# Splitting the first two rows of four residual stages during the stage before, and reserving their accumulators one by one

## The reference, cut to what matters

```python
h = h + mixed @ w_out                                         # "out":  16 rows of 128 inputs
h = h + (silu(v @ w_ffn_gate) * (v @ w_ffn_up)) @ w_ffn_down  # "down": 44 rows
...
h = h + mix @ w_out_2                                         # "out2": 16 rows
h = h + memory_cross_attention(...)                           # "xo":    4 rows
h = h + peer(...)                                             # "v0" and "v1": 64 rows each
```

## Time and profile before

| What | Value |
|---|---|
| runs shown | 4111.41, 4116.86, 4119.94 us; median 4116.86 |
| profiled execution, its own time | 4109.78 us |
| its span in the trace | 4108.1 us |
| PE busy | 3978.6 us, 97% |
| DVE busy | 2362.7 us, 58% |
| ACT busy | 2064.1 us, 50% |
| chain of work that ended last | PE 94%, DVE 3%, ACT 2%, issue 1% |
| rows in the six residual stages | 208 |

### The profile page before, as it was taken

The page is one execution under the profiler, slowest core; times in us unless marked ns, Lnnn a source line. Parts: engine busy times, 40 slices in busy tenths (PEclk is TensorE's granted clock), DMA queues, the critical chain, the costliest instruction groups (busy, mean ns, idle before and its releaser), DMA issues.

```text
span 4108.1 us, 82547 instructions
## 1 busy us (share of the span) xinstructions
PE 3978.6 (97%) x33876; PEld 3930.4 (96%) x33876; DVE 2362.7 (58%) x3414; ACT 2064.1 (50%) x3097; POOL 33.4 (1%) x61
## 2 busy tenths in 40 slices
PE   7999999999999998999999998999999999999998
PEld 6999999999999998999999898999999999999998
DVE  5655565554444456444665665897765555554555
ACT  6555554455555444444554444447764444444443
POOL 0000000000000000000000000000000000000000
PEclk9999999999999999999999999999999999999999
DMA  4545555545555554543335443555555556665553
GB/s 174 175 165 175 174 178 182 175 162 191 191 191 193 183 194 148 175 165 134 134 125 184 155 173 124 185 195 180 179 192 191 192 193 215 214 214 179 191 193 132
DMA packets 111188, 726.08 MB, mean 177 GB/s; under 512 B 11296, under 2 KB 11424, under 8 KB 29184
## 3 DMA queue, kind: packets, MB, share of 16 engines
q1 hardware_dynamic: 105904, 701.55, 49.8%
q0 software_dynamic: 5072, 21.50, 1.6%
HBM read 712.52 MB, written 10.49 MB: 176 GB/s over the span
## 4 chain that ended last, share of the span: by engine, by line
PE 94%; DVE 3%; ACT 2%; issue 1%; DMA 0%; DVEq 0%; SPq 0%; ACTq 0%
PE ps L493 19%; PE ps L501 19%; PE ps L494 19%; PE ps L550 9%; PE ps L552 9%; PE ps L557 9%; PE ps L580 1%; PE ps L981 1%; PE ps L615 1%; PE ps L522 1%; PE ps L523 1%; PE ps L524 1%; ACT wh L1043 1%; PE ps L633 1%; DVE tmp L1661 1%
## 5 line engine op out<-in xcount | busy, mean ns | idle before, releaser
L1602 DVE TENSOR_TENSOR wl<-raw,wh 128x1024 fp32r<-128x1024 f32 x1328 | 1616.8, 1225 | 1509.7 <-ACT wh L1043 1505.1
L1043 ACT ACTIVATE wh<-raw 128x1024 fp32r<-128x1024 f32 x1328 | 1402.9, 1060 | 1770.3 <-PE ps L550 625.1
L493 PE MATMUL ps<-x,wh 128*128 128x256 f32 x6784 | 1620.0, 281 | 41.6 <-DVE x L1655 25.1
L494 PE MATMUL ps<-x,wh 128*128 128x256 f32 x6784 | 1604.2, 278 | 0.0
L493 PEld LDWEIGHTS ps<-x,wh 128*128 128x128 f32 x6784 | 1283.9, 189 | 51.2 <-issue 44.8
L494 PEld LDWEIGHTS ps<-x,wh 128*128 128x128 f32 x6784 | 1283.6, 189 | 0.6
L501 PE MATMUL ps<-x,wl 128*128 128x256 f32 x6784 | 919.0, 278 | 2.9 <-DVE wl L1602 2.9
L501 PEld LDWEIGHTS ps<-x,wl 128*128 128x128 f32 x6784 | 843.2, 189 | 3.2 <-DVE wl L1602 3.1
L550 PE MATMUL ps<-xkh,wh 128*128 128x256 f32 x3328 | 783.7, 278 | 29.1 <-DVE xkl L1613 27.2
L552 PE MATMUL ps<-xkl,wh 128*128 128x256 f32 x3328 | 783.2, 278 | 0.0
L550 PEld LDWEIGHTS ps<-xkh,wh 128*128 128x128 f32 x3328 | 630.4, 189 | 30.1 <-issue 30.1
(11 more groups left out here) (340 smaller groups left out, 2190.4 us busy)
## 6 DMA issues: line engine op xcount, KB each, us to landing
raw<-in_w_in SPq DMA_DIRECT2D x184, 1024.0 KB, 4.8
raw<-in_expert_u SPq DMA_DIRECT2D x128, 1024.0 KB, 4.8
raw<-in_expert_v SPq DMA_DIRECT2D x128, 1024.0 KB, 4.8
raw<-in_w_ffn_gate SPq DMA_DIRECT2D x44, 1024.0 KB, 4.7
raw<-in_w_ffn_up SPq DMA_DIRECT2D x44, 1024.0 KB, 4.8
raw<-in_w_ffn_down SPq DMA_DIRECT2D x44, 1024.0 KB, 4.8
raw<-in_w_out SPq DMA_DIRECT2D x32, 1024.0 KB, 4.8
raw<-in_w_branch SPq DMA_DIRECT2D x16, 1024.0 KB, 4.9
```

The costliest lines, as they stand in the source:

```text
L493: begin(mm(o, wh[:, j, c], x_h[:, kc, :], start=kc == 0, stop=False), kc % 8 == 0)
L494: mm(o, wh[:, j, c], x_l[:, kc, :], start=False, stop=False)
L1043: f(wh[:, u % 4, 0:width], raw[:, ring, c:c + width], ACT.Copy).then_inc(*k.up("hi"))
L1602: v.tensor_tensor(wl[:, u % 4, 0:width], raw[:, ring, c:c + width], wh[:, u % 4, 0:width].bitcast(F32), ALU.subtract).then_inc(*k.up("lo"))
```

## The change

- `residual` on ACT and DVE takes `early=True` for `out`, `down`, `out2` and `v1`: the split of rows 0 and 1 is left out there, and a new function `early_rows` does it sooner. ACT's version waits for a new semaphore, `early_ready`, which DVE sets once some tile before the last is complete.
- `out`: DVE sets the flag before the last quarter (q = 3). ACT splits after the fourth gate tile, DVE ahead of the multiplications of `mix_in(3, 3)`. Banks of this last tile are filled and read in the order 3, 4, 5, 7. The two weight halves of this `mix_in` move behind the second and the fourth bank. The flag `masks_free` moves behind the residual stage.
- `down` and `v1`: the last turn of the loops `ffn` and `u1` on ACT and DVE is written out, and the split is in its last tile: on ACT after the gate of `ffn`, and before the last tile of `u1`; on DVE after the third (`ffn`) or first (`u1`) weight half of the last tile. In `ffn` DVE's fourth half goes behind the multiplication.
- `out2`: DVE sets the flag after `mixed_b(6)`, ahead of `scaled(1)`. ACT splits before the weight halves of u = 7, DVE before its first half of u = 7; its second half goes behind `mixed_b(7)`.
- PE (all six residual stages): instead of all eight banks ahead of the first row, each bank is reserved just before its first matmul.
- `xo` and `v0` keep the late split.

```diff
+        def mix_banks(n, q):
+
+            return (3, 4, 5, 7) if (n, q) == (3, 3) else (7, 4, 5, 3)
...
-                parts_T([(b, Y_AT[n], 4) for b in (7, 4, 5, 3)])
-                marks["wb", n, q] = k.n["full_v3"]
+                parts_T([(b, Y_AT[n], 4) for b in mix_banks(n, q)])
+                marks["wb", n, q] = k.n[f"full_v{mix_banks(n, q)[-1]}"]
...
+                        if first and t % 2 == 0:
+                            reserve(t // 2)
...
-                reserve(*range(8))
                 rows(True, False)
...
-            def residual(src, name, n, more=True, between=None):
-                act.wait_ge(*k.next("src_ready"))
+            def early_rows(src):
+
+                act.wait_ge(*k.next("early_ready"))
                 for j in range(2):
                     xsplit(src, j, k.at("hi", -4))
+
+            def residual(src, name, n, more=True, between=None, early=False):
+                act.wait_ge(*k.next("src_ready"))
+                if not early:
+                    for j in range(2):
+                        xsplit(src, j, k.at("hi", -4))
...
                     gate(3, 4 * q + t)
+                if q == 3:
+                    early_rows(mix1)
                 mixed_in(3, q)
-            residual(mix1, "out", KC)
+            residual(mix1, "out", KC, early=True)
...
                     flag("gate_ready")
+                    if last and n == 1:
+                        early_rows(hidT)
                     done_v(4 + n, i + (marks["ffn"][n] + 1))
-            residual(hidT, "down", FT)
+
+            with k.loop("ffn", act, FT // 2 - 1) as i:
+                unit_turn(i)
+            unit_turn(FT // 2 - 1, True)
+            residual(hidT, "down", FT, early=True)
...
             for u in range(4, 8):
+                if u == 7:
+                    early_rows(mix2)
                 up_done(u)
...
+                    if last and j == 7:
+                        early_rows(ag)
                     done(b)
...
-                half()
+                last = (n, q) == (3, 3)
+                if last:
+                    early_rows(mix1)
+                else:
+                    half()
                 dve.wait_ge(*k.next("gate_ready"))
-                for t, b in enumerate((7, 4, 5, 3)):
+                for t, b in enumerate(mix_banks(n, q)):
...
-                    if t == 2:
+                    if t == (1 if last else 2):
                         half()
+                if last:
+                    half()
...
             for q in range(4):
+                if q == 3:
+                    flag("early_ready")
                 for t in range(4):
                     chunk()
                 mix_in(3, q)
+
+            residual(mix1, "out", KC, early=True)
             flag("masks_free")
-
-            residual(mix1, "out", KC)
...
-                    split()
+                    half()
+                    if last and n == 1:
+                        early_rows(hidT)
+                    else:
+                        half()
...
+                    if last and n == 1:
+                        own()
+                        half()
+
+            with k.loop("ffn", dve, FT // 2 - 1) as i:
+                unit_turn(i)
+            flag("early_ready")
+            unit_turn(FT // 2 - 1, True)
+            residual(hidT, "down", FT, early=True)
...
-                split()
-                mixed_b(u)
+                if u == 7:
+                    early_rows(mix2)
+                    half()
+                    mixed_b(u)
+                    half()
+                else:
+                    split()
+                    mixed_b(u)
+                if u == 6:
+                    flag("early_ready")
...
-                    split()
+                    half()
+                    if last and j == 15:
+                        early_rows(ag)
+                    half()
```

More of the change, by code:

```diff
@@ L226, in build @@
         sem("a_ms", "a_sd", "a_y", "cmp_in", "cmp_hid", "cmp_s", "kv_ready")
-        sem("top_m", "top_e", "idx_ready", "lr_ready", "er_ready", "oh_ready", "g1_staged", "g1_out0", "g1_out1", "g1_in0", "g1_in1", "gbuf_free", "w1_free", "lam_a", "lam_b", "masks_free", "out_ready", "y_ready", "xkh_ready", "xkl_ready", "kv2_ready")
+        sem("top_m", "top_e", "idx_ready", "lr_ready", "er_ready", "oh_ready", "g1_staged", "g1_out0", "g1_out1", "g1_in0", "g1_in1", "gbuf_free", "w1_free", "lam_a", "lam_b", "early_ready", "masks_free", "out_ready", "y_ready", "xkh_ready", "xkl_ready", "kv2_ready")
         sem("spread", "a_ready")
@@ L1070, in mixed_in @@
                     meanwhile()
-                act.wait_ge(S["full_v3"], marks["wb", n, q])
+                act.wait_ge(S[f"full_v{mix_banks(n, q)[-1]}"], marks["wb", n, q])
                 half(True)
@@ L1267, in _, with unit_turn @@
                     gate(3, 4 * q + t)
+                if q == 3:
+                    early_rows(mix1)
                 mixed_in(3, q)
-            residual(mix1, "out", KC)
+            residual(mix1, "out", KC, early=True)
             norm(hT)
             split(True)
-            with k.loop("ffn", act, FT // 2) as i:
+            def unit_turn(i, last=False):
                 for n in range(2):
@@ L1447, in memory_high @@
                     high_part(row // 2, xh)
-            residual(mix2, "out2", KC, between=memory_high)
+            residual(mix2, "out2", KC, between=memory_high, early=True)
             for q in range(4):
@@ L1561, in _, with gated_rows @@
                 act.wait_ge(S[f"g1_out{turn}"], 16 * 8)
-            with k.loop("u1", act, 8):
+            def gated_rows(last=False):
                 for j in range(8):
                     b = j % 2
+                    if last and j == 7:
+                        early_rows(ag)
                     done(b)
@@ L1568, in _ @@
                     flag("gate_ready")
-            residual(ag, "v1", HALF, more=False)
+            with k.loop("u1", act, 7):
+                gated_rows()
+            gated_rows(True)
+            residual(ag, "v1", HALF, more=False, early=True)
             norm(hT, parts=False)
@@ L1614, in xsplit, with early_rows, residual @@
                                 ALU.subtract).then_inc(*k.up("xkl_ready"))
-            def residual(src, name, n, more=True, between=None):
-                flag("src_ready")
+            def early_rows(src):
                 for j in range(2):
                     xsplit(src, j)
+            def residual(src, name, n, more=True, between=None, early=False):
+                flag("src_ready")
+                if not early:
+                    for j in range(2):
+                        xsplit(src, j)
                 if between is not None:
@@ L1908, in _, with unit_turn @@
                 mix_in(3, q)
+            residual(mix1, "out", KC, early=True)
             flag("masks_free")
-            residual(mix1, "out", KC)
             norm(hT, "norm_ffn")
             split()
-            with k.loop("ffn", dve, FT // 2) as i:
+            def unit_turn(i, last=False):
                 for n in range(2):
                     split()
-                    split()
+                    half()
[3 more added lines that the diff above has]
+                        half()
                     dve.wait_ge(*k.next("gate_ready"))
@@ L2143, in memory_low @@
                     low_part(row // 2 - 1, xh, xl)
-            residual(mix2, "out2", KC, between=memory_low)
+            residual(mix2, "out2", KC, between=memory_low, early=True)
             split()
@@ L2352, in _, with gated_rows @@
             split()
-            with k.loop("u1", dve, 4) as i:
+            def gated_rows(i, last=False):
                 for j in range(16):
                     b = j % 2
-                    split()
+                    half()
+                    if last and j == 15:
+                        early_rows(ag)
+                    half()
                     if j % 8 == 0:
@@ L2365, in _ @@
                         flag("gbuf_free")
-            residual(ag, "v1", HALF, more=False)
+            with k.loop("u1", dve, 3) as i:
+                gated_rows(i)
+            flag("early_ready")
+            gated_rows(3, True)
+            residual(ag, "v1", HALF, more=False, early=True)
             norm(hT, "norm_final_2", tmp, "out_ready")
```

## The result

The changed kernel takes 4089.76 us (median; 4088.18 to 4093.04), the kernel before 4116.05 us (4111.41 to 4119.94) beside it. The ratio is 0.9939, with a 95% interval of 0.9926 to 0.9951. Timed once more beside the kernel before, it took 4092.27 against 4115.40 us, ratio 0.9944 (0.9931 to 0.9958). So it is 23 to 26 us faster; 24.7 were forecast.

A forecast was written before the change was run, and what follows sets the result against it. PE was taken as the bound, busy 3978.6 of 4108.1 us. Savings of 8.1 (`out`), 5.5 (`down`), 5.0 (`v1`) and 6.1 (`out2`) sum to 24.7 us, from a median of 4116.86 to 4092.2 us; range 4084 to 4101.

The forecast's parts named there:

- The terms of `out`, `down` and `v1`: Savings before these residual stages, from gaps and slow first halves: 8.1, 5.5 and 5.0 us.
- The second gap in `v1`: In the first row of `v1`, PE waits about 0.6 us for bank 1, which ACT's last Gelu empties.
- The term that was off: `out2`: Saving before `out2`: 6.1 us (5.1 to 6.6), with 3.0 of the 9.46 us gap staying.
- the price of the low clock: First half of `out2`: low clock after the 3.0 us gap, partly under bank waits, adds 0.5 us (0 to 1.48).
- a first half takes over 4 us: Sign of being wrong: the first half of a stage's first row exceeds 4 us.
- The two waits on banks that it expected in `out2`: First row of `out2`: PE waits for banks 2 and 3, free at 2297.1 and 2298.0, needed after 8 and 12 matmuls.
- reserving at 0: Bank-wise reserving on PE: no further gain or cost, 0 us; far end 0.1 us a wait, 3 us in all.
- The clock staying low after small gaps: Rival: first halves of `down`, `out2`, `v1` still run at 0.50, 4.4 us not won, 4096.6 us; chance 0.14.
- The stall at row 2: Rival: DVE is late and PE waits for row 2 in each stage, 1.5 us four times, 4098.2 us; chance 0.07.
- the lost lead: Rival: ACT and DVE, fewer halves ahead, delay each of 140 rows; at 0.3 us a row 4134.2 us; chance 0.02.
- the stream as the new bound: Rival: without the gaps memory can't catch up and its stream bounds, so no change, 4116.9 us; chance 0.02.
- That `out2` would keep its whole gap: Rival: `xkl` is held up in `out2` so the whole 9.46 us stays, 4098.3 us; chance 0.05.

The follow-up runs named there:

- experiment 3: The changed kernel with the banks of the last tile before `out` filled and read in the old order 7, 4, 5, 3: 4089.98 us in one run.
- experiment 5: The changed kernel with the late split back in `down` alone: 4091.64 us in one run.
- experiment 9: The changed kernel with rows 0 and 1 split early in `xo` too: 4087.70 us in one run.
- experiment 4: The changed kernel with the flag `masks_free` set ahead of `out` again: 4095.76 us in one run.
- experiment 8: The changed kernel with splits before `down` and `v1` ahead of DVE's weight half, last Gelu ahead of ACT's last half: 4086.84 us in one run.
- Experiment 7: The changed kernel with `out2` split sooner, scalings moved into its first rows and banks swapped: median 4089.34 us, ratio 0.9938 to the kernel before.
- experiment 1: The kernel before with only bank-by-bank reserving added, the split left late: 4113.83 us, ratio 0.9994.
- experiment 2: The changed kernel with all eight banks reserved ahead of the first row again: 4096.84 us, ratio 0.9951 to the kernel before.

## Why the prediction was right

**The sum.** 24.7 us were forecast, 23.1 and 26.3 measured in two timings, 23.55 at the seams. The terms of `out`, `down` and `v1` came out within 0.12 us. Part of that closeness is luck: the terms were read from the same profile that the seams are counted from, and against the second profile of the kernel before `out` gained 8.71 us, not 8.08, because its first half was slow for longer there. The same holds for the median: 4089.76 us in one timing and 4092.27 in the other, with 4092.2 forecast. The range of 4084 to 4101 held.

**What decides the start.** That the first `xkl` is what PE waits for, and that it stands behind DVE's work of the moment, was right in all four: nothing ahead in `out`, a weight half in `down` and `v1`, `scaled(1)` in `out2`. The latency of 0.68 us was too long by 0.2: the changed kernel shows 0.47. The second gap in `v1`, behind the Gelu, came nearly as forecast: 3.54 - 2.83 = 0.71 us lost, against 0.6.

**The term that was off: `out2`, 5.1 instead of 6.1 us.** The gap was 2.77 us for 3.0, and bank 3 was free when forecast, 2.7 us after PE's start. But the first half took 5.45 us, where the forecast's own times give 2302.8 - 2.90 - 2295.35 = 4.55, and the second 3.22 instead of 2.90, as the clock stayed low into it. That is 0.9 + 0.3 too long, less 0.3 for the gap. The step that failed is the price of the low clock: "Part of it lies under the waits for banks 2 and 3", put at 0.5 us. The timeline of DVE around the start and two stretches of the changed kernel:

```profile
2284.51 1.67 DVE L2175 SCALAR_TENSOR_TENSOR tmp<-memT,par,rstd 128x256 f32<-128x256 f32 x4
...
2286.22 0.42 DVE L1644 TENSOR_TENSOR xkl<-mix,xkh 128x256 fp32r<-128x256 f32 x1
...
2288.95 0.42 DVE L2127 TENSOR_TENSOR mtmp<-ps,gt_b 128x256 f32<-128x256 f32 x1
...
2286.00:2288.00 2.00, 1.30 (x6) 1.30 (x7) 1.96 (x5) 1.22 (x2) 0.00 (x0) 0.50 0.47 193
...
2290.00:2292.00 2.00, 2.00 (x12) 2.00 (x11) 2.00 (x4) 0.00 (x0) 0.00 (x0) 0.50 0.00 0
```

The clock is 0.50 up to 2292, so all 24 matmuls of the half run slow and take 5.45 us, and the banks are free when PE gets to them: the low clock hid the waits, not the waits the clock. Where it was low for less of the half, 4.3 to 4.4 us were measured (experiments 3, 5, 9). With 1.00 at the start, in experiments 4 and 8, PE waits for bank 2, 0.6 us, and never for bank 3: the forecast had both. Between profiles of kernels with these rows of `out2` unchanged the seam was 9.99 to 11.45 us, so this term is worth 5.1 to 6.6 us, by the clock, and the forecast's 6.1 lies inside. Experiment 7 shows what it could be.

**The signs of being wrong.** The forecast named "a first half takes over 4 us" as a sign that it is wrong, and `out2`'s took 5.45. The sign was badly drawn, as the forecast's own 4.55 us for that half is over 4 too. Of the other three, `v1`'s 3.54 lies a little above the 2.7 to 3.4 that it gave. The two waits on banks that it expected in `out2` didn't come in the changed kernel.

**The two parts.** The forecast took the early split as the gain and reserving at 0. Experiments 1 and 2 say it more exactly: reserving one by one is worth nothing alone, and the early split without it loses 7.3 us of its 23.55 at the seams. So the early split alone gains 16.2 us, and reserving one by one, worth nothing without it, adds 7.3. Part of the 7.3 is the low clock in `out` after a gap of 1.95 us.

**The rivals.** The clock staying low after small gaps: not seen, 2.83 us in `down` after 0.27 and no slow matmuls in `v1` after 0.27 and 0.41. By the Trainium skill's account of a clock that oscillates as PE cycles through banks (TensorE: Matmul & The Clock Gate, A second HAM failure mode: psum-queue depth-cycling) it would have been so; the trace does not agree for gaps of this size. The stall at row 2, the lost lead and the stream as the new bound: from row 1 on no half takes more than 2.72 us in any of the stages, and no wait of PE names a transfer. That `out2` would keep its whole gap: no.

**The masks, the peeled turns, the order of banks.** Moving the masks shows no gain, as costed. The order of banks before `out` is worth 0.4 us, which the sum didn't name. The peeled loop turns were not tried by themselves; PE's busy time, the same within 1 us, shows no cost of them.

## What to carry to other kernels

A wait at a seam has three layers: the operand that is late, the buffers that are reserved in one piece, and the clock afterwards. Take each from the trace, and ask of the work ahead of the late operand whether it must stand there: here the source's first rows were complete long before its last tile. When two profiles are compared, compare seams, not spans: an untouched stretch of 660 us differed by up to 9 us.

## What the runs showed of the hardware

Between 1.8 and 3.8 us the length of a gap did not tell whether the clock falls. It stayed at 1.00 after 3.77 us (experiment 5) and after 3.57 us in the first profile of the kernel before, and fell after 1.95 us (experiment 2); after 1.82 us in `xo` it did both. Where it falls, the half behind the gap takes 1.3 us longer (4.17 for 2.83, `out` in experiment 2) to 2.6 (5.45, `out2` in the changed kernel). So the forecast's way of reading it, by the nearest of two waits, 1.78 us at 1.00 and 2.82 at 0.50, does not hold in this range. The small gaps that the change leaves, 0.27 and 0.41 us, were followed by 1.00 each time. The Trainium skill (TensorE: Matmul & The Clock Gate, What's actually happening) says that the window of the monitor behind the clock runs free of the kernel's start. One program giving 656.84 and 660.38 us for the same stretch fits that, and doesn't prove it.

With the eight banks' waits ahead of the wait for `xkl`, PE's start follows the start of `xkl` by 0.68 us (0.53 in `xo`), though in `out2` the last bank was read 3.6 us before that start. Reserved one by one, it follows by 0.47 to 0.48 us at every seam where PE waits for `xkl`, in experiment 1 too, whose only edit this is. Why this is 0.2 us was not tried.
